# ConvFFN in two stages: opening, up-projection stage and round changes reordered, and TensorE's waits on low parts moved to the third of a product that uses them

## The reference, cut to what matters

```
def conv_ffn(xn, buf, w_g, w_u, w_c, b_c, w_d):
    g = xn @ w_g                                   # 1088 tokens x 1024 -> 3072
    gc, new_buf = causal_dwconv(g, buf, w_c, b_c)  # width 3
    return (jax.nn.gelu(gc) * (xn @ w_u)) @ w_d, new_buf
...
x -> x + conv_ffn(rmsnorm(x, g_ffn), ...)          # after each of the two mixers
```

## Time and profile before

| | us |
|---|---|
| median of 3 runs | 2687.48 |
| the three runs | 2686.31 to 2687.71 |
| the profiled execution, its own time | 2689.28 |
| its span from the first to the last instruction | 2687.6 |
| PE busy | 2494.0 (93%) |
| DVE busy | 1790.8 (67%) |
| ACT busy | 1149.8 (43%) |
| POOL busy | 1038.4 (39%) |

### The profile page before, as it was taken

The page is one execution under the profiler, slowest core; times in us unless marked ns, Lnnn a source line. Parts: engine busy times, 40 slices in busy tenths (PEclk is TensorE's granted clock), DMA queues, the critical chain, the costliest instruction groups (busy, mean ns, idle before and its releaser), DMA issues.

```text
span 2687.6 us, 46186 instructions
## 1 busy us (share of the span) xinstructions
PE 2494.0 (93%) x18693; PEld 2387.7 (89%) x18693; DVE 1790.8 (67%) x2118; ACT 1149.8 (43%) x1851; POOL 1038.4 (39%) x663
## 2 busy tenths in 40 slices
PE   8999998897899999988988999996999999988888
PEld 7878876697899999988988999996999999988888
DVE  6456566547687777786667434548677768777774
ACT  5575666434444444443223433434443444433331
POOL 3244332225344545452223412244535455442221
PEclk9999999998999999999999999998999999998999
DMA  5101118642223222255332211121223232274322
GB/s 177 56 24 43 42 32 283 232 151 81 73 79 109 90 94 101 82 189 185 121 112 78 57 35 52 55 90 56 94 89 106 77 106 93 99 258 136 127 81 79
DMA packets 214176, 276.98 MB, mean 103 GB/s; under 512 B 11437, under 2 KB 158998, under 8 KB 210894
## 3 DMA queue, kind: packets, MB, share of 16 engines
q1 hardware_dynamic: 212910, 271.83, 30.4%
q10 hardware_dynamic: 576, 2.10, 0.2%
q0 software_dynamic: 480, 0.11, 0.0%
HBM read 203.57 MB, written 70.43 MB: 102 GB/s over the span
## 4 chain that ended last, share of the span: by engine, by line
PE 60%; DVE 10%; issue 5%; DMA 2%; ACT 1%; POOL 1%; SPq 0%; ACTq 0%; DVEq 0%; POOLq 0%
PE psum_all L2190 46%; PE psum_all L2798 6%; PE psum_all L148 6%; DVE x_residual L2492 2%; DVE psum_all L2115 1%; DVE x_residual L2486 1%; DVE x_residual L2480 1%; DMA pair_raw_ffn<-in_w_down_dram 1%; POOL down_x_ffn L2132 1%; DVE down_x_ffn L2132 1%; DVE ffn_x_sums L2440 0%; DVE x_residual L2543 0%; PE psum_all L2850 0%; PE psum_all L2814 0%; DVE block_s L2121 0%
## 5 line engine op out<-in xcount | busy, mean ns | idle before, releaser
L2190 PE MATMUL psum_all<-ffn_x,blocks 128*128 128x272 f32 x5760 | 748.6, 291 | 65.3 <-DVE x_residual L2480 34.6
L2190 PEld LDWEIGHTS psum_all<-ffn_x,blocks 128*128 128x128 f32 x5760 | 738.2, 191 | 70.9 <-issue 55.3
L2190 PE MATMUL psum_all<-down_x_ffn,blocks_down 128*128 128x272 f32 x2880 | 395.6, 299 | 74.4 <-issue 44.4
L2190 PEld LDWEIGHTS psum_all<-down_x_ffn,blocks_down 128*128 128x128 f32 x2880 | 386.4, 199 | 80.3 <-issue 79.9
L2307 ACT COPY x_residual<-psum_all 128x544 f32<-128x544 f32 x192 | 117.8, 614 | 403.5 <-PE psum_all L2190 399.1
L2543 DVE TENSOR_TENSOR x_residual<-x_residual,psum_all 128x544 f32<-128x544 f32 (+1 forms) x224 | 178.6, 798 | 152.9 <-PE psum_all L2190 151.5
L113 POOL TENSOR_TENSOR w_lo_part<-w_raw,w_hi_part 128x1024 fp32r<-128x1024 f32 x52 | 126.9, 2440 | 356.0 <-ACT w_hi_part L97 356.0
L2480 DVE TENSOR_TENSOR x_residual<-x_residual,psum_all 128x544 f32<-128x544 f32 x144 | 130.4, 906 | 123.6 <-PE psum_all L2190 119.8
L2127 POOL TENSOR_TENSOR x_residual<-x_residual,rms_scale 128x1088 f32<-128x1088 f32 x48 | 134.8, 2809 | 180.6 <-ACT x_residual L2336 180.6
L2121 DVE TENSOR_TENSOR blocks<-psum_all,blocks 128x512 fp32r<-128x512 f32 x138 | 94.9, 688 | 118.4 <-ACT blocks L2288 118.4
L2798 PE MATMUL psum_all<-operand_a,w_hi_part 128*128 128x364 f32 (+1 forms) x672 | 169.9, 330 | 0.0
(11 more groups left out here) (372 smaller groups left out, 4835.5 us busy)
## 6 DMA issues: line engine op xcount, KB each, us to landing
staging_ffn<-hidden_spill SPq DMA_DIRECT2D x54, 816.0 KB, 6.1
hidden_spill<-x_residual SPq DMA_DIRECT2D x24, 1088.0 KB, 4.0
w_raw<-in_w_gate_dram SPq DMA_DIRECT2D x24, 1024.0 KB, 5.6
x_residual<-in_w_up_dram SPq DMA_DIRECT2D x24, 1024.0 KB, 5.2
pages<-in_cache_k_dram SPq DMA_DIRECT2D x64, 256.0 KB, 3.6
pages<-in_cache_v_dram SPq DMA_DIRECT2D x64, 256.0 KB, 5.6
x_spill<-x_residual SPq DMA_DIRECT2D x24, 546.0 KB, 5.5
x_residual<-x_spill SPq DMA_DIRECT2D x24, 546.0 KB, 5.8
```

The source lines that it names most:

```text
L2190: mm = pe.matmul(self.core.ps[:, b + h, 0:HB], wt[:, q * P:(q + 1) * P], xt[:, q, HB * h:HB * (h + 1)], start=first and at == 0, stop=at = ...
```

## The change

What it does, in five parts.

1. **Waits.** Outside job 0, the head of a product waits for the high parts only. The wait for the low weights stands at the second third, that for the low input (first job of a round) at the last third.
2. **Opening.** The weight sums of job 0 and their low parts move from GpSimd to VectorE, ahead of the residual add of tile 6 (`first_weights_dve`); ScalarE makes four high parts of weights ahead of tile 6. GpSimd keeps low parts 0, 1 and 5, the squares and its halves of T1 and T3. The sums and low parts of job 1 move from behind the opening to between its last steps. The norm's sums use bank pair `d`.
3. **Stage.** `conv_taps` is cut into two `conv_tap`; in an up job `add_out` of product 1 stands between them. The two taps of the second tile stand on either side of low part 3 and S3.
4. **First down job.** `down_first` writes out VectorE's list anew: all seven low parts of pieces, then the weights of job 25, and the last hidden tile and its four sums (before partly on GpSimd) at the very end. SyncE issues pieces 7 to 10 of the next round ahead of the last store of the hidden tile, no longer behind it.
5. **Turns.** All low parts of pieces are VectorE's; B21 and B11 follow `add_residual` 1 and 2 of the round's last job, T1 and T2 its 4 and 6, and B22, NT4 and T3 fall into the first job of the new round, whose weight sums for the next job move behind NT4.

```diff
@@ tensor
             for i in range(7):
-                pe.wait_ge(*self.lo_ready(n, i))
+                def low(s):
+                    if s == 1:
+                        pe.wait_ge(*self.lo_ready(n, i))
+                    elif m >= 0 and m % QUARTERS == 0:
+                        pe.wait_ge(*self.x_lo_done(m // QUARTERS, i))
+
+                pe.wait_ge(self.w_hi, 7 * n + i + 1)
...
                     if m % QUARTERS == 0:
-                        pe.wait_ge(*self.x_lo_done(m // QUARTERS, i))
+                        pe.wait_ge(self.x_hi, 7 * (m // QUARTERS) + i + 1)
...
-                self.multiply(pe, n, i)
+                self.multiply(pe, n, i, None, low)
@@ multiply
+            if low and q == 0 and s:
+                low(s)
@@ gpsimd
+        self.block_lo(pool, 0, 0)
+        self.block_lo(pool, 0, 1)
         self.add_squares(pool, KT - 2)
-        pool.wait_ge(*self.out.job_done(KT - 2))
-        self.first_sums(pool, "S1")
-        for i in (1, 0, 2):
-            self.block_lo(pool, 0, i)
...
-                if n == JOBS1 - 1 and i in (5, 6):
-                    self.piece_lo(pool, 0, (T2, NT4)[i - 5])
-                elif turn and i in (T2, NT4):
-                    self.piece_lo(pool, r + 1, i)
@@ Output.vector
-            if m == KT - 1:
+            if m == KT - 2:
+                self.ffn.first_weights_dve(dve)
+            elif m == KT - 1:
                 self.ffn.open_dve(dve)
@@ opening_act
+        for i in range(4):
+            self.block_hi(act, 0, i)
         self.tile_act(act, KT - 2)
-        self.block_hi(act, 0, 1)
-        self.block_hi(act, 0, 0)
@@ vector, an up job
-            self.conv_taps(dve, o, t, 0)
+            self.conv_tap(dve, o, t, 0, 1)
             self.add_out(dve, u, 1)
+            self.conv_tap(dve, o, t, 0, 0)
@@ vector, a down job
+            turn, turned = p == QUARTERS - 1 and r < ROUNDS - 1, p == 0
+            if not turned:
+                self.next_sums(dve, n + 1)
             for i in range(7):
                 self.add_residual(dve, n, i)
+                if turn and i == 1:
+                    self.piece_lo(dve, r + 1, B21)
+                elif turn and i == 2:
+                    self.piece_lo(dve, r + 1, B11)
+                elif turned and i == 1:
+                    self.piece_lo(dve, r, B22)
+                elif turned and i == 2:
+                    self.piece_lo(dve, r, NT4)
+                    self.next_sums(dve, n + 1)
+                elif turned and i == 3:
+                    self.piece_lo(dve, r, T3)
+                self.next_lo(dve, n + 1, i - (1 if turned else 0))
+                if turn and i == 4:
+                    self.piece_lo(dve, r + 1, T1)
+                elif turn and i == 6:
+                    self.piece_lo(dve, r + 1, T2)
+                if turned and i == 6:
+                    self.next_lo(dve, n + 1, 6)
@@ down_first (new, job 24)
+        self.piece_lo(dve, 0, T1)
+        self.add_residual(dve, n, 0)
+        self.add_residual(dve, n, 1)
+        self.piece_lo(dve, 0, T2)
+        self.piece_lo(dve, 0, B22)
+        self.add_residual(dve, n, 2)
+        self.piece_lo(dve, 0, NT4)
+        self.add_residual(dve, n, 3)
+        self.piece_lo(dve, 0, T3)
+        self.next_sums(dve, n + 1)
...
+        self.hidden_tile(dve, t, 0)
+        self.hidden_tile(dve, t, 1)
+        for i in (T1, T3, T2, NT4):
+            self.hidden_sum(dve, t, i)
@@ sync
         self.load_next(sp, n + 2)
+        for g in range(7, 11):
+            self.load_piece(sp, g)
         self.store_hidden(sp, PAIRS - 1)
```

223 lines of the change are left out of this document (98 added, 125 removed).

## The result

| | before | after |
|---|---|---|
| median of 4 runs | 2686.89 us | 2582.17 us |
| lowest and highest | 2680.74, 2687.71 | 2578.63, 2585.86 |
| the profiled execution, its own time | 2689.28 | 2578.63 |
| its span | 2687.6 | 2576.9 |

A forecast was written before the change was run, and what follows sets the result against it. TensorE bounds the kernel, and where it stands still it waits for VectorE's list. Savings of 17.5 + 45 + 30 + 21 = 113.5 us from 2689.3 give 2575.8, taken as a 2574 us median; range 2536 to 2612.

The forecast's parts named there:

- the upper bounds of the parts: All parts of the change at their most favourable: recorded as 157 us saved, giving 2530 us.
- Stage, 17.5: Up jobs: all 17 waits of 1.03 us on add_out go, saving 17.5 us, bounds 12 and 17.5.
- Turns, 45: Six turns between rounds: loss falls from 10.6 to 3.2 us each, 45 us saved in all.
- Opening, 30: Three waits opening each ConvFFN: first and third shrink, second grows slightly; 14.8 us per ConvFFN, 30 for both.
- First down jobs, 21: Jobs 24 to 26: 10.5 us saved per ConvFFN, 21 for both, bounds 10 and 30.
- Its larger item: Job 26's wait of 6.96 us for job 27's weights goes with 2.5 of slow pace: 9.4 saved.
- In job 24 the order by need takes out 4.08 and its 1.6 of pace: First down job: VectorE's reordered list removes a wait of 4.08 us and 1.6 of slow pace behind it.
- behind them TensorE stands about 3 us before product 3 of job 25: Two hidden tiles and four sums ahead of job 25's first add cause this wait, leaving some 1 us saved.
- one of 4.7: A single 4.7 us wait counted within the 39.3 us of 20 waits ending with add_out.
- Waits inside products, 0: 546 waits at products' second third in the ConvFFNs: satisfied ones cost nothing; bounds 0 and 0.01 us each.
- The first rival: VectorE becomes the bound at turns and in the opening: 69.5 us saved, 2618 us; chance 0.16.
- The second rival: Nearly all TensorE waits go, low parts overlapping better than added up: 148 us saved, 2539 us; chance 0.21.

The follow-up runs named there:

- the mark: The changed kernel measured once more, nothing altered, beside the runs that take a part of it: ratio 0.9606 to the kernel before, median 2576.24 us.
- tap_only: Kernel before, with only the up job's add_out of product 1 moved between the first convolution's two taps: ratio 0.9921, median 2663.81 us.
- job1_late: Changed kernel with job 1's weight sums and low parts behind the opening again, and ScalarE's high parts of them later: ratio 0.9715 to the kernel before, 2603.05 us.
- late_pieces: Changed kernel with the transfers of pieces 7 to 10 issued behind the last store of hidden tiles again: ratio 0.9699 to the kernel before, 2599.89 us.
- pool_lows: Changed kernel with the low parts of T2 and NT4 at the turns given back to GpSimd: ratio 0.9672 to the kernel before, 2590.60 us.
- best: Changed kernel plus opening without GpSimd's long operations, job 24's adds first, hidden sums on GpSimd, job 27's weights before the last store: 0.9560 to kernel before, 2563.18 us.

## Why the prediction was right, and where it was off

- **Sign, size and range.** Forecast 2574 in a range of 2536 to 2612, measured 2582.17 and, in the second comparison, 2576.24. In its own terms, on the profiled execution: 113.5 forecast, 110.7 found, of which about 108 are the change's. One recorded sum is wrong: the upper bounds of the parts (17.5, 57, 38 and 30) make 142.5 saved and 2545, not 157 and 2530. The forecast doesn't hang on it.
- **Stage, 17.5.** Shown, by the trace and by `tap_only` (21 us, with 2.8 of wait at job 1 and 1.8 of pace behind it). The rest of the stage is 13.5 us shorter in the first ConvFFN, 2.5 of them the pace behind the opening's third wait, so 11.0 against 8.75. Nine of the 17 waits stood there, so each cost about 1.2 and not 1.03: the 0.24 that the forecast took for the tail of the 48 matmuls behind one (6.24 where the pace gives 6.00) is nearly all lost as well.
- **Turns, 45.** Shown: 23.2 in the first ConvFFN against 22.5, and about 20 in the second, where one round took 67.3 us because 90 matmuls behind a wait of 1.76 took 13.03. The forecast waits were 0.7 and 1.1 with 1.4 for GpSimd; 0.45 and 1.76 stand there, at full pace but for two of the six turns, and the second is indeed for the add of product 5. The forecast did not say what engine and order are worth apart; they overlap, 5.0 and 5.4 alone.
- **Opening, 30.** Right in sum: 12.4 and 2.5 of pace in the first ConvFFN, 14.9 against 14.8, and about 14 in the second. The sum is partly luck, since the parts missed by up to 1.7 and cancel: the first wait 7.24 to 4.90 where I had 3.2 (and 2.70 in the mark, by the tie told below), the pace behind it 7.93 to 8.38 for 48 matmuls where I had 0.9 less, the second 7.28 to 6.23 where I had 7.7, the third 8.54 to none where I had 1.5. `job1_late` shows the third to be worth 10 us or more in each ConvFFN.
- **First down jobs, 21.** The mis-sized term: 7.2 and 7.0 us were saved, 14. Its larger item holds: the 9.4 of job 26 are gone, and `late_pieces` shows the place of the four transfers to be worth 24 us in all. What failed in the first ConvFFN is mostly the step "In job 24 the order by need takes out 4.08 and its 1.6 of pace". The order by need leaves 2.59 of wait in the middle of product 2, for a low part, and 1.5 of slow pace behind it; job 24 is 3.1 us shorter, not 5.7. The step "behind them TensorE stands about 3 us before product 3 of job 25" failed in place and a little in price: the wait of 3.51 stands at the head of job 25, for the add of product 5, behind low parts and weight sums, and the 54 matmuls behind it took 9.67 where 7.01 is full pace, 2.7 more. Job 25 is 5.4 us longer than before, where the sum allowed it 4.6. In the second ConvFFN the sum took job 24 to be the same as in the first, and it wasn't. The kernel before waited there ahead of product 1, which is the "one of 4.7" that the forecast read and priced nowhere; 4.34 of it is left, with 2.7 of pace behind:

```profile
2372.52 7.31 PE L2190 MATMUL psum_all<-down_x_ffn,blocks_down 128*128 128x272 f32 x36 [4.73 <-DVE x_residual L2480]
```

- **Waits inside products, 0.** Shown twice, 0.9997 alone and 0.9603 against 0.9606 within the change.
- **The first rival**, VectorE as the bound at turns, is out: no wait of 4 us stands at a turn. Its mechanism is real, as `pool_lows` shows, but costs little once only short low parts are left to GpSimd. The second rival, nearly all waits gone, wanted 148 us saved; even `best` comes to 119.

What stays open is why the two ConvFFNs differ in job 24, before and after: 4.08 ahead of product 2 and 4.73 ahead of product 1 before, 2.59 and 4.34 now. In the second one's trace a low part of 4.19 us stands on VectorE beside a gate scaling of 4.14 on GpSimd, with the add of product 1 behind it; in the first the low part takes 1.85 and the gate scaling comes later. That is what exclusion would give, but no run moved either.

## What to carry to other kernels

Look at what a waiting engine waits for before moving the wait: here most long waits were for an add that stood in the list behind work wanted later, and moving the wait did nothing while moving one add ahead of one tap gave 21 us. A gain on one engine can be taken back whole by the next transfer that lands just in time, so look at the slack of the next load, and count the bytes ahead of it on the queue beside the issues, before moving work forward. Work given to a second engine is worth its own time only if the two can run together; check the time of the first engine's operations beside it.
